# Turning the attention probabilities one half-block later and spreading a convolution over more half-blocks, in a two-layer encoder kernel on one Trainium2 core

## What is computed

```
h = rmsnorm(x, norm1_g[l]) * (1.0 + sc1) + sh1
q, k, v, ca, cb, su, gates = jnp.split(h @ w_in[l], ...)
y_attn = sliding_window_attention(q, k, v, attn_sinks[l]) @ w_attn_o[l]
y_conv = conformer_conv(ca, cb, ...)      # 31-tap depthwise conv, layernorm, silu, @ w_pw
y_ssm  = s5_ssm(su, ...)
mixed = gate_a * y_attn + gate_c * y_conv + gate_s * y_ssm
x = x + g1 * (mixed @ w_out[l])
```

## Time and profile before

| | |
|---|---|
| time, median of 3 runs | 1031.75 us (1031.64 to 1031.78) |
| the profiled execution: its own time | 1028.69 us |
| its span in the trace | 1026.9 us |
| TensorE busy (matmuls) | 946.5 us, 92% |
| VectorE busy | 669.1 us, 65% |
| ScalarE busy | 464.6 us, 45% |
| chain that ended last | TensorE 65%, VectorE 23%, ScalarE 4%, DMA 3%, issue 3% |
| mean granted TensorE clock | 0.972 of full |

### The profile page before, as it was taken

How to read it: one execution, slowest core, us unless ns; L and a number is a source line. 1 busy time by engine, 2 the same in 40 slices (tenths; PEclk the granted TensorE clock), 3 DMA queues, 4 the chain that set the end, 5 groups by cost and what they waited for, 6 DMA issues and landing times.

```text
span 1026.9 us, 16212 instructions
## 1 busy us (share of the span) xinstructions
PE 946.5 (92%) x6911; PEld 795.2 (77%) x6911; DVE 669.1 (65%) x910; ACT 464.6 (45%) x544; POOL 8.7 (1%) x11
## 2 busy tenths in 40 slices
PE   5688998999998899999998999999999799999995
PEld 2487985666776878898996997666676599999994
DVE  3783878999575485456446576899966654444445
ACT  4484135623643465545335332564264453434342
POOL 2000000000000000000000000000000000000000
PEclk9798899999999999999999999999999999999998
DMA  9955235548666446465657534454867625555521
GB/s 340 234 201 206 83 125 204 204 135 292 256 253 156 164 167 244 166 228 204 223 166 162 165 104 175 174 211 158 273 230 280 212 92 179 191 186 184 192 96 41
DMA packets 128023, 194.01 MB, mean 189 GB/s; under 512 B 30706, under 2 KB 90618, under 8 KB 121808
## 3 DMA queue, kind: packets, MB, share of 16 engines
q1 hardware_dynamic: 127608, 192.85, 55.8%
q10 hardware_dynamic: 344, 0.14, 0.1%
HBM read 191.93 MB, written 1.05 MB: 188 GB/s over the span
## 4 chain that ended last, share of the span: by engine, by line
PE 65%; DVE 23%; ACT 4%; DMA 3%; issue 3%; SPq 0%; ACTq 0%; DVEq 0%
PE bank L537 18%; PE bank L538 17%; PE bank L539 17%; DVE wlo L1316 7%; DVE yc L1597 7%; PE bank L573 3%; DMA raw<-in_w_mod 2%; PE bank L629 2%; PE bank L602 2%; ACT whi L978 1%; PE bank L652 1%; DMA raw<-in_w_out 1%; PE bank L640 1%; DVE h L1490 1%; PE bank L728 1%
## 5 line engine op out<-in xcount | busy, mean ns | idle before, releaser
L1316 DVE TENSOR_TENSOR wlo<-raw,whi 128x2048 fp32r<-128x2048 f32 x132 | 302.1, 2290 | 237.5 <-PE bank L539 191.1
L978 ACT ACTIVATE whi<-raw 128x2048 fp32r<-128x2048 f32 x132 | 252.3, 1911 | 160.0 <-DMA raw<-in_w_in 73.0
L537 PE MATMUL bank<-hhi,whi 128*128 128x256 f32 x992 | 287.5, 290 | 7.1 <-DVE hlo L1495 4.0
L538 PE MATMUL bank<-hlo,whi 128*128 128x256 f32 x992 | 282.8, 285 | 0.0
L539 PE MATMUL bank<-hhi,wlo 128*128 128x256 f32 x992 | 282.7, 285 | 0.0
L537 PEld LDWEIGHTS bank<-hhi,whi 128*128 128x128 f32 x992 | 192.4, 194 | 16.3 <-issue 10.4
L538 PEld LDWEIGHTS bank<-hlo,whi 128*128 128x128 f32 x992 | 192.6, 194 | 0.6
L539 PEld LDWEIGHTS bank<-hhi,wlo 128*128 128x128 f32 x992 | 192.4, 194 | 0.0
L537 PE MATMUL bank<-whi,bhi 128*128 128x512 f32 x304 | 121.4, 399 | 3.4 <-DVE wlo L1316 3.4
L538 PE MATMUL bank<-wlo,bhi 128*128 128x512 f32 x304 | 119.1, 392 | 0.0
L539 PE MATMUL bank<-whi,blo 128*128 128x512 f32 x304 | 118.8, 391 | 0.0
(11 more groups left out here) (247 smaller groups left out, 839.4 us busy)
## 6 DMA issues: line engine op xcount, KB each, us to landing
raw<-in_w_mod SPq DMA_DIRECT2D x48, 1024.0 KB, 7.3
raw<-in_w_ffn_in SPq DMA_DIRECT2D x44, 1024.0 KB, 5.2
raw<-in_w_in SPq DMA_DIRECT2D x38, 1024.0 KB, 5.4
raw<-in_w_ffn_out SPq DMA_DIRECT2D x22, 1024.0 KB, 5.0
raw<-in_w_out SPq DMA_DIRECT2D x8, 1024.0 KB, 6.9
raw<-in_w_in SPq DMA_DIRECT2D x16, 256.0 KB, 5.1
raw<-in_ssm_glu_b SPq DMA_DIRECT2D x4, 1024.0 KB, 5.1
raw<-in_ssm_glu_a SPq DMA_DIRECT2D x4, 1024.0 KB, 5.1
```

The source lines that it names most:

```text
L537: mm(o, w_hi, a_hi, start=start, stop=False, skip_group_check=True)
L538: mm(o, w_hi, a_lo, start=False, stop=False, skip_group_check=True)
L978: fn(whi[mi % N_HI][:, :], raw[SLOT[item]][:, :], ACT.Copy).then_inc(s_hi, 1)
L1316: V.tensor_tensor(wlo[mi % N_LO][:, :], raw[SLOT[("main", *divmod(mi, NB))]][:, :], whi[mi % N_HI][:, :].bitcast(F32), ALU.subtract).then_ ...
```

## The change

The turn of the probabilities and the product with the values come one half-block later in each of the four rounds (t = 22, 25, 28, 31 and 23, 26, 29, 32 in place of 21, 24, 27, 30 and 22, 25, 28, 31). In rounds 0 to 2 the turn now falls on the half-block of the next round's scores and stands ahead of them in `side`. The 16 convolution pieces, at t = 20, 21, 23, 24, 26, 27, 29, 30, 32, 33, 35, 36, 38, 39, 41, 42 before, are now at t = 20, 21, 23, 25, 26, 28, 30, 31, 33, 35, 36, 38, 40, 41, 43, 45. The mean moves from t = 46 to 49, the variance from 48 to 51.

```
-PROBS_LAG = 2
+PROBS_LAG = 3
 SCORES_AT = {19 + 3 * r: r for r in range(4)}
 PROBS_AT = {t + PROBS_LAG: r for t, r in SCORES_AT.items()}
 ATTEND_AT = {t + PROBS_LAG + 1: r for t, r in SCORES_AT.items()}
...
-CONV_AT = {20 + 3 * n // 2: divmod(n, 8) for n in range(16)}
-CONV_MEAN_AT, CONV_VAR_AT = 46, 48
+CONV_AT = {20 + 27 * n // 16: divmod(n, 8) for n in range(16)}
+CONV_MEAN_AT, CONV_VAR_AT = 49, 51
```

## The result

| | before | after |
|---|---|---|
| time, median | 1031.76 us | 1042.7 us (1041.22 to 1046.27) |
| ratio, 95% interval | | 1.0105 [1.0073, 1.0138] |
| profiled execution: own time, span | 1028.69, 1026.9 | 1046.27, 1044.5 |
| TensorE, VectorE, ScalarE busy | 946.5, 669.1, 464.6 | 959.2, 668.9, 465.2 |

The change costs 10.9 us.

What follows compares the result with a forecast made beforehand. VectorE was taken as pace-maker, with the convolution branch's end then holding up `cp` 0; delays of 1.9 and 4.5 us plus 2 x 1.7 us of slow clock gave +9.8 us on 1031.75, so 1041.5 us, range 1035.5 to 1045.5 us.

Steps and rivals of the forecast that it cites:

- Part 1, the turn: Turn and scores: TensorE's 7.0 us wait goes, but only VectorE's idle time is won, 2.2 us (layer 0), 0.8 (layer 1).
- Part 2, the pieces: Ahead of `ao` 0: VectorE gets there earlier but idles 1.8 us (layer 0) and 2.7 us (layer 1) for the cast.
- Part 3, the statistics: Ahead of `cp` 0: the variance's root stands behind a cast and its load; `cp` 0 starts 1.9 and 4.5 us later.
- The clock: Behind each wait ahead of `cp` 0: 3.4 us at half speed, 1.7 us of lost work per layer.
- Sum: Whole kernel: delays of 1.9 and 4.5 us plus twice 1.7 us for the clock, +9.8 us.
- The table load: Ahead of the root on ScalarE: the switch costs 1.3 us by the trace, about 2.66 us by the skill page.
- The rivals: Whole kernel: faster (chance 0.07), even at +1.9 us (0.06), slower by half at +5.3 or +6.4 (0.27), worse at +13 to +15 (0.12).
- the faster one: Whole kernel: the stall was the cost and `cp` 0 starts without a wait, -3.4 us, 1028.4 us; chance 0.07.
- 18.5 us chain: From `cp` 0's load request: load, cast, table load, root, reciprocal and product, silu and cast, low part, `wlo`, without overlap.

Runs made afterwards that it cites:

- the version with 48 and 50: The changed kernel with the mean at 48 and the variance at 50 in place of 49 and 51: 1025.16 us, ratio 0.994 to the kernel before.
- The one with 49 and 50: The changed kernel with only the variance moved, from 51 to 50, the mean staying at 49: 1033.23 us, ratio 1.0007 to the kernel before.
- pieces with 48 and 50: The changed kernel's pieces, statistics at 48 and 50, the turn as in the kernel before: 1033.56 us, ratio 1.0023 to the kernel before.
- turn with 48 and 50: The kernel before with the later turn and statistics at 48 and 50, its pieces unmoved: 1033.19 us, ratio 1.0001.
- the two kernels with spread pieces and the early turn: The changed kernel with the old turn, statistics at 49 and 51 (1053.74 us) or at 48 and 50 (1033.56 us).

## Why the prediction was right

It forecast 1041.5 us; measured were 1042.7. By its steps:

- **Part 1, the turn.** Right: the wait and the slow clock at 180 us are gone and little time is won, since VectorE has little idle time to give. Alone the turn brought 2.2 us.
- **Part 2, the pieces.** The `wlo` of `ga` 0 began at 201.56 us (200.95 predicted). The request for `ao` 0 came 21.77 us behind it in layer 0 and 19.07 in layer 1, where I took 18.85. In layer 0, 2.84 us of that are the slow clock in `ga` 0, a term that the sum did not have and that this execution alone shows; without it, 18.93. VectorE's idle time was 4.77 us instead of 1.8 for this reason, and 2.62 instead of 2.7 in layer 1. In the version with 48 and 50, where `ga` 0 ran at full clock, it was 1.51 us.
- **Part 3, the statistics.** The mechanism was right in each of its steps. `gc` 1 started 2.34 us behind its `wlo` in both layers, and the request for `cp` 0 came 8.5 us behind that, against 2.35 and 8.4. From the request to `cp` 0 it took 284.76 - 266.33 = 18.43 and 788.79 - 770.15 = 18.64 us, against 18.5. TensorE's work in that time was 14.0 us, not 13.6, so the waits were 4.4 and 4.6 us instead of 4.9. Counted from `gs` 0, `cp` 0 came 4.7 us later in layer 1 (4.5 predicted) and 4.9 in layer 0, of which 2.8 are again `ga` 0: 2.0 against 1.9.
- **The clock** was the mis-sized term: 2.8 and 1.7 us in the two `cp` 0, not 1.7 each, because in layer 0 it stayed down for 6.8 us. The other kernels with a wait ahead of `cp` 0 of over 4 us show 1.4 to 3.0 us each.
- **Sum.** 2.0 + 4.7 + 4.5 = 11.2 us with `ga` 0 taken out, against 9.8 predicted and 10.9 measured. That these two come within 0.3 us is luck in part, since the rest of the program varies by more than that from one execution to the next.
- **The table load.** 1.28 us, and the root starts 1.30 us behind the load's start, as in the rows before. The 2.66 us of the Trainium skill ("ScalarE: Activation LUTs", "What ACT_TABLE_LOAD costs") are not what this place shows.
- **The rivals.** The turning point of the faster one was the 18.5 us chain against what the request gives back. The version with 48 and 50 breaks that chain and does get faster, by 6.2 us, where the rival said 3.4. The one with 49 and 50 breaks it too and comes out even.

I missed two things. The mean at 49 stands behind a cast too, and its place costs 6.9 us once the root is ahead. And turn and pieces depend on each other. Both later expectations that added their worth (pieces with 48 and 50: 1028.4 for 1033.6; turn with 48 and 50: 1027 for 1033.2) failed.

## What to carry to other kernels

An item that is put one slot later in an engine's list takes on everything that now stands ahead of it, and a cast that waits for a load was the dear neighbour here. Before moving it, go through the list of the engine that reads its result, not only of the one that makes it; here one number less (50 for 51) is worth 10 us, and one more (48 for 49) another 7. When two moves act on the same engine's backlog, time them together too, since neither shows its worth alone.

## What was not expected of the hardware

- The clock fell behind a wait of 1.48 us ahead of `ga` 0, with short matmuls of 128x4 around it, where before a wait of 2.83 us left it at 1.00. In `glb` 0 of layer 1 the block took 9.9 us in place of 7.6 behind waits of 1.97 and 1.98 us, in the two kernels with spread pieces and the early turn; the windows behind them show the clock at 0.53 and 0.57. The length of the wait alone does not tell whether it falls: at `ga` 0, 1.48 us of waiting brought it down in after, and 1.49 us did not in the version with 48 and 50.
- Behind waits of like length (4.4 to 4.7 us ahead of `cp` 0), `cp` 0 took between 7.2 and 8.6 us, against 5.6.
- Runs of one kernel differ by some 3 to 4 us either way, and the mean granted clock goes with it: the turn alone took 1026.57 us at 0.975 and 1033.73 at 0.964. A difference of 2 us is seen only over many runs.
